# Scaling h2 ahead of its high and low split in a one-core encoder layer

## The reference, cut to what matters

```
h2 = rms_norm(x, norm2_g)                 # x * rsqrt(mean(x*x) + eps) * g
q  = h2 @ peer_wq                         # 8 heads of 128
s1 = q[first half]  . sub_k1              # 128 keys
s2 = q[second half] . sub_k2              # 128 keys
# top 16 of each half, the 256 sums, top 16 of those: 16 experts a head, softmax gates g
a  = einsum('td,thkd->thk', h2, u_tab[idx])
out = einsum('thk,thkd->td', g * gelu(a), v_tab[idx])
x  = x + out
```

## Time and profile before

| what | us |
|---|---|
| median of 3 runs | 4547.72 (4543.62 to 4548.77) |
| profiled execution, whole time | 4554.25 |
| its span on the core | 4552.4 |
| PE busy | 4373.8 |
| DVE busy | 2932.5 |
| POOL busy | 1755.5 |
| ACT busy | 1079.0 |

### The profile page before, as it was taken

How to read it: one execution, slowest core, us unless ns; L and a number is a source line. 1 busy time by engine, 2 the same in 40 slices (tenths; PEclk the granted TensorE clock), 3 DMA queues, 4 the chain that set the end, 5 groups by cost and what they waited for, 6 DMA issues and landing times.

```text
span 4552.4 us, 78733 instructions
## 1 busy us (share of the span) xinstructions
PE 4373.8 (96%) x30758; PEld 4286.7 (94%) x30758; DVE 2932.5 (64%) x4653; ACT 1079.0 (24%) x1100; POOL 1755.5 (39%) x639
## 2 busy tenths in 40 slices
PE   8999999999999999999898898999989999999999
PEld 7999999999899999999888888999989999999999
DVE  5766656577752166667999999400057777777874
ACT  3323223232211132222221221222211212221221
POOL 3333323332333344444443443454544444344420
PEclk9999999999999999999999999999999999999999
DMA  6656566564333222233333333423376777777773
GB/s 241 235 179 237 197 220 236 191 235 144 114 128 135 98 101 106 106 108 113 124 127 128 128 119 123 154 107 114 124 288 261 283 264 280 273 273 271 274 267 124
DMA packets 332183, 822.57 MB, mean 181 GB/s; under 512 B 23152, under 2 KB 230768, under 8 KB 264688
## 3 DMA queue, kind: packets, MB, share of 16 engines
q1 hardware_dynamic: 279968, 608.53, 38.2%
q0 software_dynamic: 22528, 134.30, 7.2%
q10 hardware_dynamic: 29520, 77.40, 4.4%
HBM read 734.72 MB, written 219.66 MB: 210 GB/s over the span
## 4 chain that ended last, share of the span: by engine, by line
PE 80%; DVE 8%; issue 7%; DMA 3%; POOL 1%; DVEq 1%; ACT 0%; ACTq 0%; SPq 0%; POOLq 0%
PE pair L1279 55%; PE pair L1555 21%; DMA a_el<-a_scr,a_idx 3%; DVE oh L1147 1%; DVE oh L1148 1%; PE ST L1531 1%; DVE g_st L1161 1%; PE ST L1346 1%; PE ST L1293 1%; DVE ST L1207 1%; POOL vg L505 1%; DVE oh L1146 1%; DVE xg L876 1%; PE ST L1348 0%; DVE h_lo L769 0%
## 5 line engine op out<-in xcount | busy, mean ns | idle before, releaser
L481 POOL TENSOR_TENSOR w_lo<-w_raw,w_hi 128x2048 fp32r<-128x2048 f32 x242 | 1117.4, 4617 | 1115.8 <-ACT w_hi L545 1115.8
L1279 PE MATMUL pair<-h_hi,w_hi 128*128 128x272 f32 x6656 | 1399.0, 291 | 12.6 <-issue 12.6
L1279 PE MATMUL pair<-h_hi,w_lo 128*128 128x272 f32 x6656 | 1382.0, 289 | 0.0
L1279 PE MATMUL pair<-h_lo,w_hi 128*128 128x272 f32 x6656 | 1376.8, 288 | 0.0
L1279 PEld LDWEIGHTS pair<-h_hi,w_hi 128*128 128x128 f32 x6656 | 1048.9, 189 | 20.8 <-issue 13.7
L1279 PEld LDWEIGHTS pair<-h_lo,w_hi 128*128 128x128 f32 x6656 | 1049.1, 189 | 0.0
L1279 PEld LDWEIGHTS pair<-h_hi,w_lo 128*128 128x128 f32 x6656 | 1043.9, 189 | 0.0
L545 ACT ACTIVATE w_hi<-w_raw 128x2048 fp32r<-128x2048 f32 x368 | 703.9, 1913 | 1425.1 <-PE pair L1555 861.1
L1555 PE MATMUL pair<-wt_hi,w_hi 128*128 128x416 f32 x2048 | 732.0, 357 | 48.9 <-DVE acc L1191 47.8
L1555 PE MATMUL pair<-wt_hi,w_lo 128*128 128x416 f32 x2048 | 732.1, 357 | 0.0
L1555 PE MATMUL pair<-wt_lo,w_hi 128*128 128x416 f32 x2048 | 726.4, 355 | 0.0
(11 more groups left out here) (223 smaller groups left out, 3945.3 us busy)
## 6 DMA issues: line engine op xcount, KB each, us to landing
w_raw<-w_all SPq DMA_DIRECT2D x368, 1024.0 KB
v_rows<-w_all SPq DMA_DIRECT2D x128, 1024.0 KB, 8.9
a_scr<-gb ACTq DMA_DIRECT2D x128, 272.0 KB, 2.1
g_scr<-g_st ACTq DMA_DIRECT2D x26, 1024.0 KB, 4.1
a_st<-a_scr SPq DMA_DIRECT2D x16, 1664.0 KB, 8.4
gl_st<-g_scr SPq DMA_DIRECT2D x16, 1664.0 KB
gate_scr<-zb ACTq DMA_DIRECT2D x32, 272.0 KB, 2.5
gt<-gate_scr SPq DMA_DIRECT2D x32, 272.0 KB, 3.2
```

What stands on the lines that cost most here:

```text
L481: pool.tensor_tensor(w_lo[:, slot, :], raw[:, slot, :], w_hi[:, slot, :].bitcast(F32), ALU.subtract)\
L1279: last = mm(out[:, f, :], a, b[:, k, f * HT:(f + 1) * HT], start=(x == 0 and y == 0), stop=(x == n - 1 and y == 2))
```

## The change

It has three parts.

1. h2 is multiplied by the inverse root mean square before it is split. In the output stage DVE now only writes x times norm2_g to `h2_s` (which lies where `h2_lo` will lie) and keeps the square sums. After the reciprocal, DVE multiplies each of the 16 tiles by `rs2`, ACT rounds it into `h2_hi`, and DVE takes the difference into `h2_lo`.
2. PE waits for the square sums and adds them up before the query stage. The first two query units then run side by side: for each slice k, 6 matmuls of unit 0 and 6 of unit 1, as soon as tile k of h2 is there.
3. The queries are only copied from PSUM. In `u_slot` ACT's gelu reads PSUM directly into `gb`; the copy to `ab` and POOL's multiplication are gone, and `ab_full` is now counted by the gelu.

```diff
             with pool.Fori(0, NU // 2) as v:
                 for n in range(2):
-                    pool.wait_ge(ab_full, v * 2 + (n + 1 + 2))
-                    pool.tensor_tensor(ab[:, n, :], ab[:, n, :], rs2[:, :], ALU.mult).then_inc(ab_scaled, 1)
                     lo(v * 2 + (n + U_PU + 2), n)
...
             act.activation(rs2[:, :], SV, ACT.Sqrt, scale=1.0 / DM, bias=sm[:, S_EPS:S_EPS + 1]).then_inc(ostd_ready, 1)
+            for k in range(KD):
+                act.wait_ge(h2_scaled, k + 1)
+                act.activation(h2_hi[:, k, :], h2_s[:, k, :], ACT.Copy).then_inc(h2_rounded, 1)
...
                 act.wait_ge(unit_done, m + (1 + NZ + NO + NQ))
-                act.activation(two(ab[:, n, :]), PV[n], ACT.Copy).then_inc(ab_full, 1)
+                act.wait_ge(a_stored[n], v * 16 + 1)
+                act.activation(two(gb[:, n, :]), PV[n], ACT.Gelu).then_inc(ab_full, 1)
                 hi(v + (U_PU // 2 + 1), n)
-                act.wait_ge(ab_scaled, m + 1)
-                act.wait_ge(a_stored[n], v * 16 + 1)
-                act.activation(gb[:, n, :], ab[:, n, :], ACT.Gelu).then_inc(gelu_done, 1)
-                act.wait_ge(gelu_done, m + 1)
+                act.wait_ge(ab_full, m + 3)
                 act.dma_start(a_scr[bass.ds(m, 1)].rearrange("a p n -> p (a n)"), gb[:, n, :]).then_inc(a_stored[n], 16)
...
-                    own.by(V.tensor_scalar(hhi, x2[:, n, :], g2, None, ALU.mult))
                     own.by(V.tensor_tensor(osq[:, :], x2[:, n, :], x2[:, n, :], ALU.mult))
+                    own.by(V.tensor_scalar(h2_s[:, bass.ds(ct, 1), :].rearrange("p a n -> p (a n)"), x2[:, n, :],
+                                           par[:, bass.ds(ct + P_G2, 1)], None, ALU.mult))
                     settle()
-                    V.scalar_tensor_tensor(h2_lo[:, bass.ds(ct, 1), :].rearrange("p a n -> p (a n)"), x2[:, n, :], g2,
-                                           hhi.bitcast(F32), ALU.mult, ALU.subtract).then_inc(h2_ready, 1)
                     own.by(V.tensor_tensor(osum[:, :], osum[:, :], osq[:, :], ALU.add))
...
             V.reciprocal(rs2[:, :], rs2[:, :]).then_inc(rs2_ready, 1)
             dve.wait_ge(rs2_ready, 1)
+            for k in range(KD + 1):
+                if k < KD:
+                    V.tensor_tensor(h2_s[:, k, :], h2_s[:, k, :], rs2[:, :], ALU.mult).then_inc(h2_scaled, 1)
+                if k > 0:
+                    dve.wait_ge(h2_rounded, k)
+                    V.tensor_tensor(h2_lo[:, k - 1, :], h2_s[:, k - 1, :], h2_hi[:, k - 1, :].bitcast(F32), ALU.subtract)\
+                        .then_inc(h2_ready, 1)
...
-                    V.tensor_tensor(two(qp[:, bass.ds(v * 2 + n, 1), :].rearrange("p a n -> p (a n)")), PV[n], two(rs2[:, :]),
-                                    ALU.mult).then_inc(qp_ready, 1)
+                    V.tensor_copy(two(qp[:, bass.ds(v * 2 + n, 1), :].rearrange("p a n -> p (a n)")), PV[n])\
+                        .then_inc(qp_ready, 1)
...
-            def rms2():
-                pe.wait_ge(osum_ready, 1)
-                spread(S, ones, osq).then_inc(ostat_ready, 1)
-
-            pe.wait_ge(h2_ready, KD - 1)
+            pe.wait_ge(osum_ready, 1)
+            spread(S, ones, osq).then_inc(ostat_ready, 1)
+
             for n in range(2):
                 pe.wait_ge(lo_ready, n + 1 + U_PQ)
                 pe.wait_ge(x2_ready, n + 1 + NO)
-                hooks = {7: rms2, KD - 2: lambda: pe.wait_ge(h2_ready, KD)} if n == 0 else None
-                product(PV[n], n, 0, range(KD), h2_hi, h2_lo, hooks).then_inc(unit_done, 1)
+            for k in range(KD):
+                pe.wait_ge(h2_ready, k + 1)
+                for n in range(2):
+                    wh, wl = (w[:, n, k * P:(k + 1) * P] for w in (w_hi, w_lo))
+                    for y, (a, b) in enumerate(((wh, h2_hi), (wh, h2_lo), (wl, h2_hi))):
+                        for f in range(2):
+                            last = mm(PV[n][:, f, :], a, b[:, k, f * HT:(f + 1) * HT],
+                                      start=(k == 0 and y == 0), stop=(k == KD - 1 and y == 2))
+                    if k == KD - 1:
+                        last.then_inc(unit_done, 1)
```

## The result

| what | before | after |
|---|---|---|
| median, us | 4547.72 (11 runs, 4539.33 to 4556.68) | 4561.42 (11 runs, 4550.59 to 4568.71) |
| ratio to before, 95% | | 1.0032 [1.0021, 1.0043] |
| profiled execution, us | 4554.25 | 4568.46 |
| its span, us | 4552.4 | 4566.6 |

The change makes the kernel 13.7 us slower by the medians. The forecast was 14.2 slower, 4562. The interval of the ratio is 9.6 to 19.6 us, so that the two numbers lie 0.5 apart is luck, and it doesn't say that the terms of the sum were right. I compared the two traces stretch by stretch. A stretch goes from one event to another that both kernels have. The numbers are differences of start times in the two profiled executions.

The account below looks back on a forecast made before the run. PE was taken as the bound, busy 4373.8 of 4552.4 us, with DVE setting the pace in the gates stage. 18.8 - 4 - 0.6 = 14.2 us slower: 4562 on the median, range 4552 to 4571.

Parts of the forecast that it names:

- The query stage's start: Start of the query stage: first matmul 12.0 us later, net 8.6, plus 5.95 and 4.2, together 18.8 us lost.
- the old wait: PE's wait inside query unit 0 for the late sum of squares; its going was to give back 3.4 us.
- the common end: First two query units end 0.75 us apart, so the third waits 5.95 us for its weights.
- the clock: Half clock after the two new PE waits: 2.2 and 2.0 us lost; rival of no fall 4557.7, chance 0.08.
- The copy's race: End of output stage: DVE's copy to osq starts 0.22 us ahead of POOL's split and takes 0.4, not 4.50.
- the rival: Copy to osq still held behind POOL's split: 4.8 us on top, time 4566.7, chance 0.10.
- The feed: Query pair: DVE needs 1.3 to 1.45 us a slice, PE 1.50; rival of DVE as bound 4566, chance 0.08.
- The gates stage: 52 u_tab units paced by DVE: 45 more let L1147 slip ahead of the split, 0.11 us each, put at 4 gained.
- The start of the v_tab stage: Last store of gb goes out some 0.65 us earlier, so POOL waits less; 0.6 us gained.
- The multiplication: u_tab units: removing POOL's multiplication, 1.38 us a unit, is worth nothing, since it ran while ACT was still rounding.
- The rival on the other side: Gates stage gives time back: 0.2 us a unit, 4555, chance 0.10; over 0.35, chance 0.04; limit 81 less, 4485.

Follow-up runs that it names:

- a_filled: Changed kernel with unread matmuls filling PE's three new waits (24 before the sum of squares, 50 behind it, 42 behind the pair); 4554.12 us, ratio 1.0011.
- a_staggered: Changed kernel with slices 0 to 7 of the first two query units side by side, then 8 to 15 of unit 0, then of unit 1; 4556.89 us, ratio 1.0019.
- a_copy_held2: Changed kernel with an unread DVE addition ahead of the copy of the square sums, so the copy starts behind POOL's split; 4570.16 us, ratio 1.0050.
- a_serial: Changed kernel with the first two query units one after the other instead of side by side; 4559.69 us, ratio 1.0034.
- a_pool_mult: Changed kernel with an unread POOL multiplication put back ahead of each split of the u_tab weights; 4563.27 us, ratio 1.0026.
- a_split_timed: Changed kernel with POOL's gates-stage split waiting until PE has finished the next unit's even group; 4468.90 us, ratio 0.9837.
- a_split_nomult_b: Kernel before with the timed split and its own ACT order, POOL's multiplication left out, so ab isn't scaled; 4459.53 us, ratio 0.9805.
- a_all: Changed kernel with the timed split, the staggered first two query units, and filling matmuls around the sum; 4466.73 us, ratio 0.9826.
- b_split_timed: Kernel before with POOL's split timed as in a_split_timed, its multiplication staying ahead of the wait; 4499.37 us, ratio 0.9896.
- a_split_mult: a_split_timed with an unread POOL multiplication put back ahead of the timed split in each u_tab unit; 4504.08 us, ratio 0.9906.

## Why the prediction was right

**The query stage's start.** Forecast: +18.8, measured +18.14. By its terms: PE's first query matmul 11.64 us after the last x2 (now 11.49; it had been 0.20 ahead of it); 3.4 of the old wait given back (it is gone); the common end 5.95 (6.00); the clock 4.2 (3.8, by the count above and by a_filled). Of the two clock losses the first was put too high, 2.2 against 1.3, and the second too low, 2.0 against 2.5, within the range of 0 to 3 for each; the sum was helped by the two errors offsetting each other. The other traces with after's instructions took up to 58.66, which is the forecast 18.8. The a_staggered kernel shows that the common end is the mechanism behind the second wait.

**The copy's race.** Forecast: won by 0.22 us; it was won by 0.53: DVE's first operation behind x2 started 0.76 after it and not 0.98, and the steps from there to the copy took 0.09 less. The split stood 3.40 behind x2 in both kernels. a_copy_held2 puts the rival's price at 5.9 to 6.6 us, not 4.8: the rival left out what the granted clock adds, above all a sum that runs at 0.50 itself (2.18 us against 1.43). The Trainium skill, page SBUF — State Buffer, section on its two separate sides, says of the port pair that VectorE and GpSimd share that whichever starts first gets it for the whole instruction and the other fully blocks. The traces agree for this copy: 0.44 us when it started first and 4.62 when it started 0.23 us behind the split. They don't agree for a lead under 0.08 us, by the start that a row gives: most operations with such a lead were held (the counts stand above). So the argument from the earlier trace rows for winning the race, an operation 0.06 ahead that ran in 0.35, was weak, and the operation of the earlier trace rows that started 0.05 ahead and took 4.74 spoke against it; the forecast margin of 0.22 and the measured one of 0.53 both lie beyond that.

**The feed.** Forecast 1.3 to 1.45 us a slice on DVE, under PE's 1.50; measured 1.27. No wait was seen within the pair. a_serial, in which PE needs a tile every 0.75, shows the waits that appear when DVE is the slower one.

**The gates stage.** Forecast: 45 more units slip, -4 us, perhaps in one slot only. It was one slot only: 26 units gain 0.20, more than the 0.11 I had counted, and the 26 of the other slot lose 0.09, which I had not counted. That these make 2.9 and lie near the 4 is in part luck. The half that I got right for a stated reason is that slot 0's wait stands by itself. The gelu from PSUM took 0.625, the same as the copy, and not 0.64, so the part of my reasoning by which a slower gelu would shift both slots was wrong.

**The start of the v_tab stage.** Forecast: the store 0.65 earlier, 0.6 gained. The store went out 2.3 us earlier, and the first gather of `a_el` 0.68, since POOL then had no wait left. So the size was right, and the time of the store was not; how much of the 0.68 reaches PE doesn't stand out from the spread of that stretch.

**The multiplication.** "Delayed nothing" was right for the change as it is (at most 0.6 us by a_pool_mult), and misleading beyond it: it cost nothing because of where it fell. With the split moved, it costs 46 us on the kernel before. The change's third part is what made the largest gain in this study possible, though by itself it is worth 3 us; moving the multiplication instead was not tried.

**The rival on the other side** (the gates stage giving it back) put 81 us as the limit if PE's wait went wholly. That the change would not do it was right. The wait did go in a_split_timed, and was worth 89 us. I had seen the 4.6 us stall and argued only that the change leaves it there.

**What the agreement doesn't show.** The profiled execution came out at 4568.46 where 4568.4 was forecast. Two stretches for which nothing was forecast, +4.3 and -4.6, cancel in it. By the medians the interval is 9.6 to 19.6 us, so they bear out the sum but none of its smaller terms; the start stretch and the gates stage are borne out by their traces.

Open remains whether the scaling could be kept off the start of the query stage while the gelu still reads PSUM: a_split_nomult_b, without either, has 39.8 us there and 4459.53 in all, but leaves the scaling of the products out. Its ratio, 0.9805 [0.9778, 0.9832], can't be told from a_all's 0.9826 [0.9811, 0.9842]. No kernel that does both was tried.

## What to carry to other kernels

When VectorE and GpSimd both work from SBUF, look for the VectorE row that is ten times its usual length, and see which of its neighbours read PSUM: starting the GpSimd operation beside those was worth 89 us of 4561, while the change as written moved 14. A cost of nothing that was read from one schedule holds for that schedule only, so ask of every operation on GpSimd what it would hold if the pattern around it moved. And when two units are interleaved because their input comes slowly, let them end apart, or the preparation of both next ones comes due at once.

## What the runs showed of the hardware

- The clock fell in some executions and not in others behind the same short wait. In three of the 14 traces (a_serial, b_split_timed, a_split_nomult_b) it fell at the score matmuls that follow the query stage, after a PE wait of 0.93 or 0.94 us. In a_serial:

```profile
1622.51 4.41 PE L1506 MATMUL ST<-ksb,qp 64*128 64x128 f32 x32 [0.93 <-DVE qp L1030]
```

```profile
1616.00:1622.50 6.50, 5.58 (x45) 5.35 (x43) 0.72 (x1) 0.89 (x1) 0.27 (x1) 1.00 0.46 161
1624.90:1631.70 6.80, 6.80 (x31) 6.58 (x31) 4.71 (x15) 0.00 (x0) 3.22 (x1) 0.50 0.37 112
```

  It costs 3.1 us each time (the first u_tab product comes 20.99 us after the last copy of queries instead of 17.90; on the kernel before 19.63 or 19.62 instead of 16.54; the 1.4 between the two kernels is the gelu's table load ahead of that row, and no delay of PE). The other 11 traces have the same short wait there and no fall. What decides it stays open; it may be one source of the few us by which runs of one kernel differ.
- How long the clock stayed at 0.50 after the same two waits (3.40 and 6.69) was not the same: until 2.9 us into the pair in after, 3.3 in a_split_mult, 4.6 in a_pool_mult, 5.4 in a_split_timed and 6.1 in a_staggered.
- A one-hot operation of VectorE had to start some 0.1 us ahead of GpSimd's split, by the starts in the rows, to run in its usual 0.34 us. With a lead of 0.003 to 0.074 us 237 were held (the one at 2216.78 in after has 0.06 and took 4.73), and only 15 with a lead of 0.039 to 0.066 ran freely. In a_split_mult the one at 2300.19 started 0.04 ahead of GpSimd's multiplication and took 1.22.
- A gelu that reads PSUM takes as long as a copy from it, 0.625 us for 128 x 544, and one from SBUF 0.646.
- In slot 0 of after a wait stands in an instruction of its own ahead of the gelu, and the gelu starts 0.085 us later against DVE than in slot 1. The 26 units of that slot were 0.20 us shorter than before.
- VectorE operations that read PSUM weren't held by GpSimd's split: the copy of 128 x 512 took 1.07 us beside it (a_split_timed) and 1.08 without it (after), while a one-hot operation of 0.34 us that started ahead of or during the split took 2.71 to 4.74.
